# Time mixing: both dense pieces of a chunk's step stand behind the product for U, none behind the one for R

## What is computed

```python
def step(s, inp):
    r_t, w_t, k_t, v_t, kk_t, a_t = inp
    sa = jnp.einsum('bhvk,bhk->bhv', s, -kk_t)
    s = (s * w_t[:, :, None, :] + sa[..., None] * (kk_t * a_t)[:, :, None, :]
         + v_t[..., None] * k_t[:, :, None, :])
    return s, jnp.einsum('bhvk,bhk->bhv', s, r_t)
```

## Time and profile before

| | |
|---|---|
| runs | 5924.08, 5916.66, 5916.29 us |
| median | 5916.66 us |
| profiled execution | 5915.66 us |
| its span | 5913.9 us |
| mean granted TensorE clock | 0.990 |
| TensorE matmuls busy | 5771.2 us, 98% of the span |
| VectorE busy | 3824.7 us, 65% |
| ScalarE busy | 2289.4 us, 39% |
| GpSimd busy | 489.0 us, 8% |

### The profile page before, as it was taken

How to read it: one execution, slowest core, us unless ns; L and a number is a source line. 1 busy time by engine, 2 the same in 40 slices (tenths; PEclk the granted TensorE clock), 3 DMA queues, 4 the chain that set the end, 5 groups by cost and what they waited for, 6 DMA issues and landing times. The chain is left out here.

```text
span 5913.9 us, 112816 instructions
## 1 busy us (share of the span) xinstructions
PE 5771.2 (98%) x48599; PEld 5619.0 (95%) x48599; DVE 3824.7 (65%) x4811; ACT 2289.4 (39%) x2840; POOL 489.0 (8%) x324
## 2 busy tenths in 40 slices
PE   7999999999999999989999999999999999999999
PEld 7888889999999999989999999999999999999998
DVE  5565652323237643256876678777777888888998
ACT  3333331222223332122234444333335556556555
POOL 0000000000000000000016661111110000000000
PEclk9999999999999999999999999999999999999999
DMA  3111112222223443321324445554545433435542
GB/s 102 37 51 39 49 40 103 108 87 108 86 90 131 156 130 131 115 86 59 107 100 158 160 165 153 150 149 142 155 129 182 147 106 114 147 111 149 169 128 84
DMA packets 374407, 682.04 MB, mean 115 GB/s; under 512 B 219616, under 2 KB 234976, under 8 KB 346464
## 3 DMA queue, kind: packets, MB, share of 16 engines
q1 hardware_dynamic: 366928, 656.81, 33.5%
q10 hardware_dynamic: 7056, 19.00, 0.8%
HBM read 562.37 MB, written 113.37 MB: 114 GB/s over the span
## 5 line engine op out<-in xcount | busy, mean ns | idle before, releaser
L2724 PE MATMUL ps<-va_h_high,va_v_high 128*128 128x288 f32 x3584 | 1056.3, 295 | 10.3 <-DVE va_h_low L140 7.6
L2726 PE MATMUL ps<-va_h_high,va_v_low 128*128 128x288 f32 x3584 | 1057.7, 295 | 0.0
L2725 PE MATMUL ps<-va_h_low,va_v_high 128*128 128x288 f32 x3584 | 1056.5, 295 | 0.0
L2724 PEld LDWEIGHTS ps<-va_h_high,va_v_high 128*128 128x128 f32 x3584 | 673.4, 188 | 11.1 <-DVE va_v_low L140 7.8
L2726 PEld LDWEIGHTS ps<-va_h_high,va_v_low 128*128 128x128 f32 x3584 | 673.4, 188 | 0.0
L2725 PEld LDWEIGHTS ps<-va_h_low,va_v_high 128*128 128x128 f32 x3584 | 673.3, 188 | 0.0
L140 DVE TENSOR_TENSOR ah_ul<-ah_u,ah_uh 128x1024 fp32r<-128x1024 f32 (+1 forms) x288 | 435.1, 1511 | 212.8 <-ACT ah_uh L2278 160.5
L1145 PE MATMUL ps<-rwkv_hn_high,rwkv_wh 128*128 128x288 f32 x1664 | 492.9, 311 | 7.0 <-PEq L225 7.0
L140 DVE TENSOR_TENSOR rwkv_wl<-ret_w,rwkv_wh 128x2048 fp32r<-128x2048 f32 (+1 forms) x138 | 260.7, 1890 | 369.2 <-ACT rwkv_wh L1246 304.5
L1146 PE MATMUL ps<-hn_low,rwkv_wh 128*128 128x288 f32 x1664 | 470.5, 298 | 0.0
L2104 PE MATMUL ps<-hn_high,ah_uh 128*128 128x288 f32 x1536 | 431.9, 297 | 5.0 <-DVE ah_ul L140 4.8
(11 more groups left out here) (488 smaller groups left out, 14839.0 us busy)
## 6 DMA issues: line engine op xcount, KB each, us to landing
va_v<-peer_v SPq DMA_DIRECT2D x96, 1024.0 KB, 5.5
ah_u<-peer_u SPq DMA_DIRECT2D x160, 512.0 KB, 6.3
ah_u<-peer_u SPq DMA_DIRECT2D x48, 1024.0 KB, 5.1
ret_w<-w_ret SPq DMA_DIRECT2D x47, 1024.0 KB, 4.8
h_kept<-ah_h SPq DMA_DIRECT2D x128, 288.0 KB, 2.3
gates<-ah_stage SPq DMA_DIRECT2D x12, 3072.0 KB, 9.7
ah_hidden<-h_kept SPq DMA_DIRECT2D x60, 576.0 KB, 4.9
ah_v<-peer_v SPq DMA_DIRECT2D x30, 1024.0 KB, 4.9
```

The source lines that it names most:

```text
L2724: pe.matmul(z, ah[:, r, f], th[:, q, r, :], start=begin, stop=False, skip_group_check=True)
L2725: pe.matmul(z, ah[:, r, f], tl[:, q, r, :], start=False, stop=False, skip_group_check=True)
L2726: done = pe.matmul(z, al[:, r, f], th[:, q, r, :], start=False, stop=r == R - 1, skip_group_check=True)
```

## The change

The two products R and U had one piece each behind them. Now R has none, and U has two. U's product is thus issued as soon as `rn` is there, with nothing between R and it, and the two pieces stand between U's product and the wait for `uu`. The number of pieces per pair stays 48, and the second tile ends in the fill of U of chunk 5.

```diff
         after = {"w": 2, "a": 2, "g": 2, "ss": 8, "bon": 5, "x": 2, "sY": 2, "sU": 2, "sV": 1, "sS": 6}
-        after.update({x: 1 for x in chain if x[0] in "RU"})
+        after.update({x: 2 for x in chain if x[0] == "U"})
         points = ["w", "a", "g", "ss", "bon", "x"] + [x[0] for x in plan] + chain + ["sY", "sU", "sV", "sS"]
```

## The result

The changed kernel's median is 5939.42 us (six runs, 5934.89 to 5944.5) against 5917.16 us (six runs, 5916.29 to 5924.08): ratio 1.0037, 95% interval 1.0024 to 1.005. It is slower by 22 us. The profiled execution took 5934.89 us, the shortest of the six.

The account below looks back on a forecast made before the run. TensorE was taken as the bound, hardly ever stopping in the chain of chunks. Open wait minus removed piece plus 0.79 per chunk gave 21.8 us, on the 5916.66 median 5938.5 us, range 5932 to 5948.

Parts of the forecast that it names:

- Term 1: Behind R in each chunk: the piece there goes, taking away 0.99 us, 1.07 in chunk 7.
- Term 2: Behind U: a second joined piece costs 0.79 us, not 1.00, so 0.20 is won per chunk.
- Term 3: Between R and U: open wait for the negation; chunk 0 0.45 us, 1–4 0.53, 5–6 0.38, 7 1.07.
- 2.72 us a pair: The eight chunks of a pair summed: chain longer by 2.72 us, in 8 pairs 21.8 us.
- The bounds around term 3: Unshown price of a wait right behind small matmuls, chunks 0 to 6: -3 us to +6 us in all.
- About 30 us in all: Sign in the changed profile: TensorE's idle time waiting for the negation, 64 waits, about 30 us.
- That the clock falls within the chains: Within the chains the clock falls to 1.2 GHz; half the chunks affected gives 109 us, 6047; chance 0.02.
- That the loss would be absorbed at the heads of the pairs: At pair heads, TensorE's 2.52 us wait takes up the loss in 7 pairs, leaving 4.2 us, 5921; chance 0.05.
- The faster case: Right behind R: an open wait under 0.20 us lets the saving win, up to 12.8 us, 5904; chance 0.03.
- the low parts' offsets: Weight preparation in VectorE's queue keeps its place behind S; negation starts 0.27 us in (chunks 1–4), 0.81 (chunk 7).

## Why the prediction was right

The forecast was 5938.5 us, measured were 5939.42; the loss of 22.3 us between medians stands against a sum of 21.8. That the two agree within 1 us is in part luck, since the interval of the ratio reaches from 14 to 30 us. What bears the forecast is that the steps agree term by term:

- Term 1, the piece behind R takes 0.99 us: as in the rows, and gone.
- Term 2, two pieces 1.79 and so 0.20 won: 1.77 in chunk 1. The kernel with both pieces behind R fits with the same 0.20: 0.38 - 0.20 gives the 0.18 to 0.19 by which its steps grew. The reason given, that the slow first matmul and the tail are paid once, can be read in the trace of before, in the two pieces of the earlier trace rows:

```profile
883.29 0.40 PE L625 MATMUL ps<-rwkv_hn_high,rwkv_wh 128*128 128x288 f32 x1
883.54 0.29 PE L626 MATMUL ps<-hn_low,rwkv_wh 128*128 128x288 f32 x1
883.66 0.30 PE L625 MATMUL ps<-rwkv_hn_high,rwkv_wh 128*128 128x288 f32 x1
...
883.93 0.42 PE L629 MATMUL ps<-rwkv_hn_high,rwkv_wl 128*128 128x288 f32 x2
884.19 0.29 PE L625 MATMUL ps<-rwkv_hn_high,rwkv_wh 128*128 128x288 f32 x1
...
884.72 0.43 PE L629 MATMUL ps<-rwkv_hn_high,rwkv_wl 128*128 128x288 f32 x2
885.08 0.33 PE L647 MATMUL ps<-rwkv_rn,rwkv_bb 64*64 64x64 f32 x4
```

  The first matmul takes 0.25 us to the next one and a following one 0.12 to 0.13. The last two take 0.36 to the small product and 0.26 where a second piece follows. Together that is 0.22 us.
- Term 3, the open wait: taken as 0.45, 0.53, 0.38 and 1.07. A step holds one open wait and one second piece, so it grows by what was worked out for its second chunk: 0.32 to 0.35 into chunks 1 to 4 (expected 0.33), 0.19 into chunks 5 and 6 (0.18), 0.78 into chunk 7 (0.79).
- 2.72 us a pair: 2.74 measured in the first pair, 2.79 on average over the eight.
- The prediction speaks of 16 pieces per pair. Those are the pieces of the chain; a pair has 48. The sum does not depend on it.
- The bounds around term 3: neither was needed. The way from the negation's start to U's was 0.27 to 0.28 us (173.84 to 174.11, 170.04 to 170.32), against 0.26 taken, with no price of a restart on top.
- "About 30 us in all" of idle time: 31.5.

The rivals. That the clock falls within the chains did not happen; the granted clock was 1.00 in every one of the eight, of which these are the first and the last:

```profile
169.50:202.90 33.40, 28.98 (x386) 23.68 (x387) 11.38 (x32) 5.47 (x14) 0.32 (x2) 1.00 0.09 33
...
872.70:906.00 33.30, 28.91 (x386) 23.60 (x387) 11.28 (x32) 5.32 (x12) 0.00 (x0) 1.00 0.15 51
```

TensorE was busy 29 of 33 us here and idle for 0.33 to 1.0 us once per chunk. What the Trainium skill tells in TensorE: Matmul & The Clock Gate, section A second HAM failure mode, about short idles that make the clock swing, did not show in these chains.

That the loss would be absorbed at the heads of the pairs did not happen either. The waits of TensorE for ScalarE's copy of the transposes, first before, then after:

```profile
PE ps L647 <- ACT rwkv_tok L574: 18.5, 7, 3.3
```

```profile
PE ps L647 <- ACT rwkv_tok L574: 19.6, 7, 3.5
```

There are seven waits as before, and in sum they are no shorter. The prediction had them unchanged; why they are 1.1 us longer stays open. The load in front of them moves with the chain, as argued from the earlier trace rows. In the changed kernel:

```profile
234.57 2.28 DVE L140 TENSOR_TENSOR rwkv_wl<-rwkv_w,rwkv_wh 128x1024 fp32r<-128x1024 f32 x1
...
236.88 0.33 SPq L403 DMA_DIRECT2D rwkv_w<-w_rkv  x1
```

The load is issued at 236.88 instead of 233.19, 3.7 us later: the 0.9 by which the first chain began later, and the 2.7 that it lost. The faster case needed an open wait under 0.20 us; the shortest was 0.38. With useful work in that wait the rest of it is 0.15, and then the order by itself comes out about even, as worked out above.

What the prediction did not say is how the loss divides. It named the low parts' offsets but treated them as given. By the steps they are 4 x 0.15 + 0.68 = 1.3 us a pair, 10 us of the 22, which the medians bear out (22.3 less 10.9 is 11.4).

## What to carry to other kernels

Cover belongs on the wait that ends last, and what sets its length is the whole queue of the other engine, not the one instruction that is waited for: here a 0.22 us negation stood behind 0.69 or 1.22 us of weight preparation. Before pieces of dense work are taken from a wait, count its length from the last instruction in front of it to the first behind it, and look for small independent products that can stand there instead. Joining two dense pieces won 0.20 us here and opened a wait of at least 0.38, so it could not pay by itself, and with two small products in that wait it about broke even. And when several moves are made at once, run the ones that help the old order too in the old order, or the gain is put down to the wrong one.

## What the runs showed that I had not expected

The heads of the pairs last either about 64 or about 66 us by the copies of U (65.64, 65.87, 64.15, 66.02, 64.22, 66.29 and 66.49 from one pair's sample rows to the next pair's chunk 0, in the kernel before). The difference goes with the granted clock after the wait of TensorE for ScalarE's copy: it fell to 0.50 after five of the seven waits (2.52, 2.46, 2.55, 2.57 and 3.26 us) and stayed at 1.00 after the other two (2.48 and 2.65), and those two heads are the short ones. In the changed kernel it fell after three of the seven, which are also its three longest heads (65.87, 65.28 and 66.55). Two such waits of the kernel before, of 2.52 and 2.48 us, the second in this row of the timeline,

```profile
437.28 0.33 PE L647 MATMUL ps<-rwkv_eye,rwkv_bb 64*64 64x64 f32 x4 [2.48 <-ACT rwkv_tok L574]
```

and the stretches behind them, where the last but two numbers are the granted clock:

```profile
242.00:244.00 2.00, 2.00 (x32) 2.00 (x30) 0.92 (x4) 0.61 (x2) 0.00 (x0) 0.50 0.00 0
...
438.00:440.00 2.00, 2.00 (x56) 2.00 (x54) 1.40 (x6) 0.80 (x3) 0.00 (x0) 1.00 0.00 0
```

After one, TensorE ran at 1.2 GHz and got through 32 small matmuls in 2 us; after the other, of nearly the same length, it stayed at 2.4 GHz and did 56. With both pieces behind R one such wait was 3.51 us and that head took 68.95, of which 0.8 is the second piece ahead of the copy. The seven heads together are 458.7, 462.0, 461.5 and 459.9 us in the four kernels with the old order, whose heads do the same work. With seven heads and about 2 us for each fall of the clock, this could be much of the spread of the runs of a kernel, which is not shown, since only one execution of each has a trace. Whether the head's wait can be taken away was not tried.
